# Attention values by pairs of query blocks, results transposed four at a time, the exponential's table loaded after each square root, and VectorE's steps in another order

## What is computed

```python
for i in range(S // Q_BLOCK):                  # blocks of 128 queries
    end = (i + 1) * Q_BLOCK
    s = jnp.einsum("bqhcd,bkhcd->bhcqk", q_blk, k_pre) * scale
    bias = jnp.where(dist >= 0, -slopes * dist, -jnp.inf)
    p = jax.nn.softmax(s + bias, axis=-1)
    attn = p[:, :, 0] - lam * p[:, :, 1]
    outs.append(jnp.einsum("bhqk,bkhe->bqhe", attn, v_pre))
o = jnp.concatenate(outs, axis=1)
o = rmsnorm(o, subln_g) * (1.0 - lambda_init)  # over the 128 values of a head
x = x + o.reshape(B, S, V_WIDTH) @ w_o
```

## Time and profile before

| | us |
|---|---|
| runs shown, median | 2520.71 |
| runs shown, lowest to highest | 2511.6 to 2520.91 |
| the profiled execution | 2519.2 |
| its span | 2517.4 |
| TensorE busy in the span | 2394.2 |
| VectorE busy | 1425.8 |
| ScalarE busy | 783.4 |
| GpSimd busy | 63.0 |

### The profile page before, as it was taken

The page is one execution under the profiler, slowest core; times in us unless marked ns, Lnnn a source line. Parts: engine busy times, 40 slices in busy tenths (PEclk is TensorE's granted clock), DMA queues, the critical chain, the costliest instruction groups (busy, mean ns, idle before and its releaser), DMA issues.

```text
span 2517.4 us, 27701 instructions
## 1 busy us (share of the span) xinstructions
PE 2394.2 (95%) x11247; PEld 1962.5 (78%) x11247; DVE 1425.8 (57%) x2167; ACT 783.4 (31%) x1367; POOL 63.0 (3%) x51
## 2 busy tenths in 40 slices
PE   6995889999999999999999999889999999999998
PEld 5883668888788888877777777778788888888888
DVE  6999599997556444456565555554733233333234
ACT  5211432222534222334444444453421111111122
POOL 0000000000000000021011011000000000000000
PEclk9997999999999999999898989999999999999999
DMA  3110223333223333321011101111111111111111
GB/s 122 50 42 25 67 70 98 96 89 100 84 84 109 101 90 97 94 71 34 26 34 34 33 10 42 42 55 40 42 54 43 55 57 45 51 51 44 57 42 76
DMA packets 278012, 154.67 MB, mean 61 GB/s; under 512 B 5669, under 2 KB 273278, under 8 KB 277886
## 3 DMA queue, kind: packets, MB, share of 16 engines
q1 hardware_dynamic: 277886, 152.90, 20.6%
HBM read 145.54 MB, written 7.34 MB: 61 GB/s over the span
## 4 chain that ended last, share of the span: by engine, by line
PE 84%; DVE 11%; ACT 3%; issue 1%; DMA 0%; SPq 0%; DVEq 0%; ACTq 0%
PE ps L1650 26%; PE ps L1523 19%; PE ps L1525 18%; PE ps L1524 18%; DVE cacc L1108 2%; PE ps L1506 2%; DVE cvA L1108 2%; ACT sc L901 1%; DVE Wl L1287 1%; PE ps L1580 1%; DVE Wl L1028 1%; DVE sc L1340 1%; ACT ATh L914 1%; DMA xrow<-in_x_dram 0%; ACT L901 0%
## 5 line engine op out<-in xcount | busy, mean ns | idle before, releaser
L1523 PE MATMUL ps<-Sh,Wl 128*128 128x512 f32 x1616 | 662.7, 410 | 23.3 <-DVE Sl L1140 9.9
L1525 PE MATMUL ps<-Sh,Wh 128*128 128x512 f32 x1616 | 637.8, 395 | 0.0
L1524 PE MATMUL ps<-Sl,Wh 128*128 128x512 f32 x1616 | 637.7, 395 | 0.0
L1523 PEld LDWEIGHTS ps<-Sh,Wl 128*128 128x128 f32 x1616 | 308.7, 191 | 103.7 <-issue 34.1
L1525 PEld LDWEIGHTS ps<-Sh,Wh 128*128 128x128 f32 x1616 | 308.1, 191 | 66.9
L1524 PEld LDWEIGHTS ps<-Sl,Wh 128*128 128x128 f32 x1616 | 308.9, 191 | 60.9 <-issue 3.6
L1028 DVE TENSOR_TENSOR Wl<-raw,Wh 128x1024 fp32r<-128x1024 f32 (+2 forms) x238 | 280.3, 1178 | 124.9 <-ACT Wh L719 123.2
L719 ACT ACTIVATE Wh<-raw 128x1024 fp32r<-128x1024 f32 (+2 forms) x238 | 240.8, 1015 | 296.5 <-DMA raw<-in_ffn_w_dram 137.5
L1650 PE MATMUL ps<-Sh,Wl 128*128 128x512 f32 x688 | 212.7, 390 | 2.5 <-DVE Sl L1255 2.4
L1650 PE MATMUL ps<-Sl,Wh 128*128 128x512 f32 x688 | 211.9, 389 | 0.0
L1650 PE MATMUL ps<-Sh,Wh 128*128 128x512 f32 x688 | 211.8, 389 | 0.0
(11 more groups left out here) (186 smaller groups left out, 3338.0 us busy)
## 6 DMA issues: line engine op xcount, KB each, us to landing
raw<-in_ffn_w_dram SPq DMA_DIRECT2D x148, 512.0 KB, 3.8
raw<-in_pw_w_dram SPq DMA_DIRECT2D x32, 512.0 KB, 3.9
raw<-in_ffn_w_dram SPq DMA_DIRECT2D x32, 448.0 KB, 3.6
raw<-in_ffn_w_dram SPq DMA_DIRECT2D x24, 384.0 KB, 3.4
xrow<-in_x_dram SPq DMA_DIRECT2D x8, 512.0 KB, 7.6
raw<-in_w_q_dram SPq DMA_DIRECT2D x8, 512.0 KB, 4.8
raw<-in_w_k_dram SPq DMA_DIRECT2D x8, 512.0 KB, 5.8
raw<-in_w_v_dram SPq DMA_DIRECT2D x8, 512.0 KB, 4.1
```

The lines of the kernel that those rows point to most:

```text
L1523: pe.matmul(dst, ll, rh, start=start, stop=False)
L1524: pe.matmul(dst, lh, rl, start=False, stop=False)
L1525: return pe.matmul(dst, lh, rh, start=False, stop=stop)
```

## The change

1. **Values by pairs.** `values(h, pair)` stands in rows 2, 4, 6 and in row 0 of the next head. The blocks of V are the stationary operand, and the weights of two query blocks move, 256 columns at once; the last product of a pair, which only the second block needs, has 128. The result is the output transposed: the 128 values on the partitions.
2. **Results four at a time.** After two pairs bank 7 is full. ScalarE copies it to `ob` (`out_copy`, rows 4 and 0), TensorE transposes its four blocks into a bank of the rotation (`out_turn`, rows 5 and 1, key `"y"` in the plan), ScalarE copies that to `orow` (`out_rows`) and squares the four rows there (`out_squares`). The softmax share is no longer in the copy but goes into the squares' scale and, by one more small multiply, into `out_norm`. `orow` has one buffer instead of two, so `out_rows` waits for the store of the head before.
3. **Table.** `out_root` is followed by an exponential of one column that nothing reads. The root stands in row 1 (and row 5 of heads 6 and 7) instead of rows 0 and 4.
4. **VectorE's order.** `out_norm` and the low parts of weight blocks stand behind `score_rows` in rows 0, 2 and 6 instead of at the ends of rows 1, 5 and 6.
5. **Scores of row 1** stand in row 0 behind the filler and the last pair's values. One operand turn moves from row 2 to row 3 of head 7, and the last one a result later.

```diff
 OPERAND_AT = {(LAST - 1, 5): ((0, LA), (1, LA)), (LAST - 1, 6): ((2, LA), (3, LA)),
               (LAST - 1, 7): ((4, LA), (5, LA), (6, LA)), (LAST, 0): ((0, LB), (1, LB), (2, LB)),
-              (LAST, 1): ((3, LB), (4, LB), (5, LB)), (LAST, 2): ((6, LB),), (LAST, 7): ((7, LA),)}
+              (LAST, 1): ((3, LB), (4, LB), (5, LB)), (LAST, 3): ((6, LB),), (LAST, 7): ((7, LA),)}
...
-OPERAND_END = min(2 * KC, len(results_through_row(TB - 1)) + 2)
+OPERAND_END = min(2 * KC, len(results_through_row(TB - 1)) + 3)
...
 def row_parts(h, i):
 
     for part in range(4):
         if part == 1:
+            if i == 1 and h:
+                yield ("y", h - 1, 1), 0, 1
+            if i == 5:
+                yield ("y", h, 0), 0, 1
             yield ("w", h, i, 0), 0, 1
...
+    yield ("y", LAST, 1), 0, 1
...
-        orow = [at(f"orow{r}", [P, TB, P], F32, G_AT + 40 * KB + r * 4 * KB) for r in range(2)]
+        orow = at("orow", [P, TB, P], F32, G_AT + 40 * KB)
+        ob = at("ob", [P, HT], F32, G_AT + 44 * KB)
+        ojunk = at("ojunk", [P, 4, P], F32, G_AT + 46 * KB)
...
-            def out_row(h, i):
-
-                t = TB * h + i
-                o = ps[:, 7, i % 4 * P:(i % 4 + 1) * P]
-                act.wait_ge(pv_mm, t + 1)
-                if i == 0 and h >= 2:
-                    act.wait_ge(o_out, 16 * (h - 1))
-                act.activation(orow[h % 2][:, i, :], o, ACT.Copy, scale=shares(h, i)[:, 0:1])
-                act.activation(o, o, ACT.Square, scale=shares(h, i)[:, 0:1],
-                               accum_out=oss(h, i, i + 1)).then_inc(osq_ok, 1)
+            def out_copy(h, hf):
+
+                act.wait_ge(pv_mm, 4 * h + 2 * hf + 2)
+                if h or hf:
+                    act.wait_ge(y_tr, 2 * h + hf)
+                act.activation(ob[:, :], ps[:, 7, :], ACT.Copy).then_inc(ot_ev, 1)
+
+            def out_rows(h, hf):
+
+                act.wait_ge(y_tr, 2 * h + hf + 1)
+                if h == LAST:
+                    act.wait_ge(o_tr, OPERAND_TURN[LAST - 1, hf] + 1)
+                elif h:
+                    act.wait_ge(o_out, 16 * h)
+                act.activation(flat(orow[:, 4 * hf:4 * hf + 4, :]), ps[:, BANK["y", h, hf], :],
+                               ACT.Copy).then_inc(orow_ok, 1)
+
+            def out_squares(h, hf):
+
+                act.wait_ge(orow_ok, 2 * h + hf + 1)
+                for i in range(4 * hf, 4 * hf + 4):
+                    act.activation(ojunk[:, i % 4, :], orow[:, i, :], ACT.Square, scale=shares(h, i)[:, 0:1],
+                                   accum_out=oss(h, i, i + 1)).then_inc(osq_ok, 1)
 
             def out_root(h, i0, i1):
                 act.wait_ge(osq_ok, TB * h + i1)
                 act.activation(oss(h, i0, i1), oss(h, i0, i1), ACT.Sqrt, bias=eps, scale=1.0 / P).then_inc(ostd_ok, 1)
 
+                act.activation(spare, eps, ACT.Exp)
+
             def operand_high(k, hf):
...
                 weights_split(h, i, 0)
-                if i:
-                    out_row(h, i - 1)
-                elif h:
-                    out_row(h - 1, TB - 1)
+                if i == 0 and h:
+                    out_copy(h - 1, 1)
+                if i == 4:
+                    out_copy(h, 0)
+                if i == 1 and h:
+                    out_rows(h - 1, 1)
+                if i == 5:
+                    out_rows(h, 0)
                 if i < TB - 1:
                     exps(t + 1, 0)
                     exps(t + 1, 1)
@@ -951,12 +984,13 @@
                     v_split(h, i)
                 if i >= 4:
                     weights_split(h, i, 1)
-                if i == 0 and h:
+                if i == 1 and h:
+                    out_squares(h - 1, 1)
                     out_root(h - 1, 4 if h == LAST else 0, TB)
-                if i == 4 and h >= LAST - 1:
-                    out_root(h, 0, 4)
-                if h == 0 and i == 0:
-                    att_split(1, K_R)
+                if i == 5:
+                    out_squares(h, 0)
+                    if h >= LAST - 1:
+                        out_root(h, 0, 4)
                 if i == 1 and not last:
                     att_split(h + 1, V_R)
...
             att_split(1, Q_R)
             exps(0, 0)
             exps(0, 1)
+            att_split(1, K_R)
             for h in range(HEADS):
                 for i in range(TB):
                     row(h, i)
-            out_row(LAST, TB - 1)
+            out_copy(LAST, 1)
+            out_rows(LAST, 1)
+            out_squares(LAST, 1)
...
             def out_norm(h, i0, i1, turn):
 
-                o = orow[h % 2][:, i0:i1, :]
+                o = orow[:, i0:i1, :]
                 dve.wait_ge(ostd_ok, turn + 1)
                 dve.reciprocal(oss(h, i0, i1), oss(h, i0, i1)).then_inc(orec_ok, 1)
-                dve.wait_ge(orec_ok, turn + 1)
+                dve.wait_ge(orec_ok, 2 * turn + 1)
+                dve.tensor_tensor(oss(h, i0, i1), oss(h, i0, i1), first_shares(h, i0, i1),
+                                  ALU.mult).then_inc(orec_ok, 1)
+                dve.wait_ge(orec_ok, 2 * turn + 2)
                 dve.tensor_tensor(o, o, oss(h, i0, i1).unsqueeze(2).to_broadcast([P, i1 - i0, P]),
                                   ALU.mult).then_inc(o_ev, 1)
...
+                if i == 0 and not last:
+                    att_lo(h + 1, K_R)
+                if i == 2 and not last:
+                    att_lo(h + 1, V_R)
+                if i == 6 and h < LAST - 1:
+                    att_lo(h + 2, Q_R)
+                if i == 2 and h:
+                    out_norm(h - 1, 4 if last else 0, TB, h if last else h - 1)
+                if i == 6 and h >= LAST - 1:
+                    out_norm(h, 0, 4, h if h == LAST - 1 else h + 1)
                 evacuate(h, i, 0)
                 weights_low(h, i, 0)
                 evacuate(h, i, 1)
...
                 evacuate(h, i, 3)
-                if i == 1 and h:
-                    out_norm(h - 1, 4 if last else 0, TB, h if last else h - 1)
-                if i == 5 and h >= LAST - 1:
-                    out_norm(h, 0, 4, h if h == LAST - 1 else h + 1)
-                if h == 0 and i == 0:
-                    att_lo(1, K_R)
-                if i == 1 and not last:
-                    att_lo(h + 1, V_R)
-                if i in (5, 6) and h < LAST - 1:
-                    att_lo(h + 2, Q_R + i - 5)
                 for k, hf in OPERAND_AT.get((h, i), ()):
...
-            def values(h, i):
-
-                t = TB * h + i
-                qs = slice(i % 2 * P, (i % 2 + 1) * P)
+            def values(h, pair):
+
+                i = 2 * pair + 1
+                q0 = pair % 2 * 2 * P
                 pe.wait_ge(tr_ev, SPLIT_TURN["w", h, i, i // 4] + 1)
-                if i in (0, 4):
-                    pe.wait_ge(tr_ev, SPLIT_TURN["v", h, i // 4] + 1)
-                if t:
-                    pe.wait_ge(osq_ok, t)
+                if pair % 2 == 0:
+                    pe.wait_ge(tr_ev, SPLIT_TURN["v", h, pair // 2] + 1)
+                    if h or pair:
+                        pe.wait_ge(ot_ev, 2 * h + pair // 2)
                 for j in range(i + 1):
-                    ins = product(ps[:, 7, i % 4 * P:(i % 4 + 1) * P], ATh[:, j, qs], ATl[:, j, qs], Vh[:, j, :],
-                                  Vl[:, j, :], j == 0, j == i)
+                    c0 = P if j == i else 0
+                    ins = product(ps[:, 7, q0 + c0:q0 + 2 * P], Vh[:, j, :], Vl[:, j, :],
+                                  ATh[:, j, c0:2 * P], ATl[:, j, c0:2 * P], j == 0, j == i)
                 ins.then_inc(pv_mm, 1)
+
+            def out_turn(h, hf):
+
+                key = "y", h, hf
+                pe.wait_ge(ot_ev, 2 * h + hf + 1)
+                bank_free(key)
+                for j in range(4):
+                    ins = transpose(ps[:, BANK[key], j * P:(j + 1) * P], ob[:, j * P:(j + 1) * P])
+                ins.then_inc(y_tr, 1)
...
-                if i < TB - 1:
+                if 0 < i < TB - 1:
                     scores(t + 1)
                 fill(h, i, 0)
-                if i:
-                    values(h, i - 1)
-                elif h:
-                    values(h - 1, TB - 1)
+                if i == 0 and h:
+                    values(h - 1, 3)
+                if i == 0:
+                    scores(t + 1)
+                if i in (2, 4, 6):
+                    values(h, i // 2 - 1)
+                if i == 1 and h:
+                    out_turn(h - 1, 1)
+                if i == 5:
+                    out_turn(h, 0)
...
-                    values(LAST, TB - 1)
+                    values(LAST, 3)
+                if u == OUT_DONE + 6:
+                    out_turn(LAST, 1)
```

More of the change, by code:

```diff
@@ L365, in trunk @@
         neg_lam = small[:, 1:2]
+        spare = small[:, 3:4]
         sub_g = small[:, 2:3]
@@ L385, in shares, with first_shares @@
             return stats[:, h % 2 * 2 * TB + 2 * i:h % 2 * 2 * TB + 2 * i + 2]
```

(11 more changed lines are left out.)

## The result

The changed kernel takes 2449.94 us (median of 4 runs, 2449.82 to 2450.98) against 2520.24 us before in the same session (2511.6 to 2520.91): a ratio of 0.973, 95% interval 0.9708 to 0.9751. The profiled execution took 2450.04 us with a span of 2448.3; 69.2 us less than the profiled one before. The forecast was 2447.0, its range 2432 to 2488.

A forecast was written before the change was run, and what follows sets the result against it. TensorE, busy for 95% of 2517.4 us, was taken as the bound. From 2519.2 us, values took off 32.0, waits 17.7 and the clock 22.8, giving 2447 us, range 2432 to 2488.

The forecast's parts named there:

- Values on TensorE: Attention stage: wider value matmuls save 4.75 us a head, transposes take back 0.75; 32.0 us less over eight heads.
- Row 2's and the boundary's waits: Waits of 2.83 us in row 2 and 2.22 us at the head's boundary both go.
- the table's early return: Row 1, ScalarE: the exponential's 1.29 us load moves behind the square root, off the chain ending in row 2's wait.
- Row 3: Heads 1 to 6: a new wait of 1.6 us for VectorE's weights, 9.6 us in all.
- Row 5: No wait forecast here: rows 4 to 6 were said to keep over 1 us of slack.
- Row 7: Without values as cover, its wait becomes 1.2 us, before 0.51; six heads, 7.5 us.
- Heads 6 and 7: Their own waits go from 11.2 to 10.7 us together, and they keep their lower clock.
- The clock: Pairs of clock drops in heads 1, 3 and 5 go: 22.8 us less.
- No drain behind a table load: ScalarE: no 1.38 us drain per load; with it, row 3 waits 2.8 us longer, the sum 17 us worse.
- The rival that the clock still drops: Attention heads: waits still lower the clock, giving 2470 us; chance 0.30.

The follow-up runs named there:

- e1: Changed kernel with each paired value product cut back into two of 128 columns: 2485.2 us.
- b2: Kernel before with the change's VectorE order and its move of one operand turn from row 2 to row 3 of head 7: 2489.4 us.
- e2: Changed kernel without the early exponential behind the square root, so the table loads only where the next row of weights needs it: 2436.1 us.
- b1: Kernel before with one addition, the early exponential behind the square root: 2497.0 us.
- e4: Changed kernel with the next row's scores back at the start of row 0, ahead of the filler and the last values: 2480.5 us.
- e6: Changed kernel, early exponential kept, with ScalarE's output rows ahead of the weights' split and squares and root behind all splits: 2426.8 us.
- e8: The kernel of e6 without the early exponential: 2427.8 us.
- b3: Kernel before with one move, the next row's scores put behind row 0's filler and values: 2492.6 us.
- e5: Changed kernel with VectorE's old order, low parts of the next operands and normalization in their old places: 2491.2 us.

## Why the prediction was right, step by step

The forecast missed by 2.9 us. Its mechanism is what the runs show: narrow value matmuls, two waits in each head and the drops with them. That the sum came so close is luck in part, for some of its terms missed by more, in both directions.

- **Values on TensorE**, forecast 32.0 us, ledger 28.2. The width's worth was under-sized: 5.0 us a head instead of 4.75, as e1 shows. My 0.109 us came from a run of 18 matmuls from its very start; e1's, from within a run, are 0.1115. What the transposes take back was under-sized too. Compared where the clock was at its full level, a head's busy time fell from 62.15 (b2, which has before's matmuls) to 58.46: net 3.7. So 1.3 went back, not 0.75. Two groups of four transposes, at 0.43 to 0.44 each (1393.54 to 1393.98 and 1421.25 to 1421.68), make 0.87 of that; the other 0.4 I haven't placed.
- **Row 2's and the boundary's waits** went as forecast. That the table's early return had a part in it is wrong (e2, b2): VectorE's order is enough, to 0.31 us in b2. Alone, the early load takes away half of row 2's wait (b1).
- **Row 3**: forecast 1.6 us in heads 1 to 6, measured 1.23 in heads 1 to 5 (6.1 us in all, not 9.6), for in head 6 the wait of 2.81 us named below comes first. TensorE came 12.5 us after row 1's transposes, as worked out. The weights were there at 13.6, the early end of my 13.8 to 15.0: the squares took longer (0.39 from one to the next, not 0.34), but VectorE's last step only 0.75, with GpSimd's next block at 1410.73, after it.
- **Row 5** was missed: 0.57 us in seven heads, 4.0 in all. A projection bank is freed by `out_rows` (L946), which ScalarE does behind the weights' split (0.50) and which takes 0.59. I had said that rows 4 to 6 keep their slack, and followed only the weights, not the banks.
- **Row 7**: forecast 1.2, measured 1.07 in heads 0 to 5, 6.4 us. (Six times 1.2 is 7.2; the sum had 7.5.)
- **Heads 6 and 7**: forecast 10.7 us of their own waits. In the trace their waits make 15.7, row 5's 0.57 among them. The long ones are 2.81 at 1526.54, then 1.22, 1.77, 1.62 and 0.38 in rows 6 and 7, and 4.68 in head 7. The 2.81 is V's low part, which in head 6 TensorE uses third and which I had put into row 2 without asking whether the last head's order wants it sooner. Waits in all: forecast 17.7 less, measured 13.1 less (45.5 to 32.4).
- **The clock**: forecast 22.8 us, ledger 29.0. The pairs of drops went, as said; by half their length they are worth 3 x 17.1 / 2 = 25.6. I had taken the price from the heads' lengths in the earlier trace rows, but each long drop begins 1.2 us before its head does (1203.6 against 1204.8), so those 1.2 us stood in the even heads that I compared with. Heads 6 and 7 win 3.4 more, for 17.1 us at the lower clock have become 10.2. This is the largest error of the sum, and it makes good what the values and the waits lacked: (-28.2 - 13.5 - 29.0) against (-32.0 - 17.7 - 22.8).
- **No drain behind a table load**: 1.29 and 1.30 us from load to next instruction again (1398.50 to 1399.79, 1400.11 to 1401.41), as the earlier trace rows had it. The Trainium skill (ScalarE: Activation LUTs, What ACT_TABLE_LOAD costs) adds a drain of 1.38 us to each load, and the trace doesn't agree.

The rival that the clock still drops was one step away: e4 shows that with the scores in their old place it does, and half of its time at the lower clock makes 15.4 of e4's 30.6 us.

## What to carry to other kernels

Before an instruction is placed early to be out of the way, look at what stands behind it in its queue: here a 1.3 us table load cost 14 us of the total where a split was queued behind it, and nothing once the splits went first. Work that frees a bank or feeds another engine's queue goes ahead of work that nobody waits for (squares, root), and a wait should be followed to banks as well as to data. Where the clock reacts to waits, a wait of 2 us can cost 4, and gains of single edits need not add, so price the edit in the kernel in which it will stand.

## What the hardware did that I had not expected

- **The same gap lowers the clock for very different times.** In b2 the boundary wait is 2.24 us in heads 1 to 6, and the drops with it last 10.2, 3.4, nothing, nothing, 13.7 and 3.4 us. Head 3 (without one) and head 5 (with the long one) of b2:

```profile
1338.00:1402.70 64.70, 62.15 (x369) 51.18 (x370) 40.51 (x86) 31.57 (x80) 7.90 (x5) 1.00 0.12 33
1467.40:1538.10 70.70, 68.15 (x371) 56.11 (x369) 40.77 (x86) 31.60 (x80) 7.91 (x5) 0.91 0.11 31
```

- In heads 1 to 5 of all these kernels no wait under 2.2 us had a drop with it, and waits up to 2.83 us stood without one (at 1443.75). In heads 6 and 7 shorter ones did: a single one of 1.94 us in e6 (at 1580.91, the drop from 1581.5), while the same 1.94 us in e8 (at 1582.57) had none; in e2 two waits of 1.68 and 0.72 us, 1.4 us apart (3.4 us from 1556.6), and in b3 one of 1.00 us at 1653.72, soon after one of 2.16 us that had its own. What decides between a short, a long and no drop is left open; no run here varied a gap's place alone.
- A drop cost half its length where it could be checked: 1.7 us for 3.4 in e4's heads. Lower clock that falls into a wait costs nothing more, as e5's ledger shows.
